# A mixture-of-experts decoder step: the routing block is put in another order

## The chip, the cores and the metric

One core of a Trainium2 chip runs the whole program. The metric is the time on the device of one execution, in microseconds; three runs of the kernel before gave a median of 1024.52 us (1024.07 to 1025.87).

The core has five engines that run their own instruction lists side by side and meet at semaphores: TensorE (PE in the profile; its weight loads are PEld), VectorE (DVE), ScalarE (ACT), GpSimd (POOL) and SyncE (SP), which here only issues DMAs. PSUM, where matmul results land, has eight banks; the kernel calls them `bank[:, 0..7, :]`.

## The reference

One step of a one-layer decoder: 256 tokens of a prompt and 8 sample tokens. Attention and a state-space branch are merged, projected and added to the residual; then a mixture of experts with a shared expert follows. The change lies between the merged branches and the experts:

```python
m = merged @ p['w_out']
x = x + g1 * rms_norm(m, p['g_post_mix'])
h = rms_norm(x, p['g_pre_ffn']) * (1 + sc2) + sh2
scores = sigmoid(h @ p['w_router'])          # 64 experts, in 8 groups of 8
biased = scores + p['b_router']              # the 4 best groups by their two best, then 6 experts
# w = scores of the 6, normalised, times 2.5
routed = sum over the chosen experts of w * (silu(h @ gate_e) * (h @ up_e)) @ down_e
shared = (silu(h @ w_gate_s) * (h @ w_up_s)) @ w_down_s
x = x + g2 * rms_norm(routed + shared, p['g_post_ffn'])
```

`rms_norm` needs the sum of squares over the 1024 channels of a token. All is float32. An expert has 3.15 MB of weights (2.1 MB gate and up, 1.05 MB down), and all 64 are read.

## The kernel before, in words

The program is a row of blocks. In each, every engine has its list; at the end of a block each engine drains (a `DRAIN` at the block's own line in the profile), and the next block starts for all when the last has. Three blocks matter: the merge (L1397), the **routing block** (L1580) and the **expert block** (L1951).

**Routing block.** Tokens are in three tiles: tile 0 and tile 2 of the router (in the code `j` = 0 and 1) are the prompt's two halves of 128, and tile 1 of the router are the 8 samples.

- TensorE projects (L1621): for each `j`, two halves of 512 output channels, one bank each, eight k-steps. The samples have their own projection (L1654, L1660) and sums of squares (L1628) ahead and between.
- For each `j` ScalarE squares the 1024 channels of a token with a running sum and takes the root (L1710, L1712); VectorE takes the reciprocal, scales and adds the residual (L1762 to L1765); ScalarE squares again; VectorE scales and shifts (L1770 to L1773). That is `h2`, tokens in partitions.
- TensorE turns `h2` in 128 x 128 pieces into banks 6 and 7 (L1634), ScalarE copies them to `h2t` (L1733, L1744), TensorE multiplies by the router's weights (L1639), ScalarE applies the sigmoid (a table switch ahead of it, L1736).
- VectorE's `route` (L1790 to L1823) finds groups, experts and ranks by max-8 and match-replace instructions and leaves a `key` per token and expert, tile 0 and the samples in one call and tile 2 in a second. TensorE turns the keys so that experts lie in partitions (L1690, L1691, L1696). `take_list` (L1832, L1838) then takes the 32 largest keys of each expert in four rounds of eight, on 64 partitions for tile 0 and samples, later on the other 64 for tile 2. The two lists are interleaved, multiplied by a parity column (L1854) and turned into slot tables (L1698, L1703, L1857 to L1865).
- Between these TensorE computes the shared expert's gate and up products in pieces (`shared`, L1646): for the first 128 tokens (`shared(.., 0, P)`, four pieces of 16 matmuls) and for the other 136 (four more). Silu and a product follow (L1749, L1868).
- GpSimd stores `h2` and the samples' rows to DRAM (L1605 to L1609), waits for those stores and for the tables, and issues the first two gathers (L1537), each of the 128 tokens of an expert pair.
- SyncE loads weights of the experts 0 to 4 into five slots. Experts 0 and 1 at once; the others when their space is free: after the last projection (L1586 on, `t_done`), after `h2` is done (`h2_ready`), and expert 4's gate and up weights after the second last shared piece has been computed (`sgu_done`).

**Expert block.** For each expert TensorE turns gathered tokens (L2038), multiplies by gate and up (L2128), by down (L2054), and adds the weighted rows (L2065). SyncE loads expert e + 5 when expert e has been multiplied (L1527, L1532). The order of the work is written out by hand everywhere.

Of the kernel before, what the change touches and what calls it, by code (L numbers as in the profile page):

```python
# [16 lines left out]
ALU = mybir.AluOpType  # L17
ACT = mybir.ActivationFunctionType
AX = mybir.AxisListType

P = 128
# [89 lines left out]
for _name, _n in (("ident", P), ("ones", P), ("eps", 1), ("causal_t", P), ("before", P), ("mask", P), ("cos", T), ("sin", T),  # L111
                  ("valid", NT), ("later", NBLK - NE),
                  ("count", MAXOVER), ("same_head", NH), ("code", NT), ("parity", 2), ("pair", NE // 2)):
    CONSTS[_name] = (_at, _at + _n)
    _at += _n
# [11 lines left out]
def build(nc, io):  # L127
    with ExitStack() as top:
# [1360 lines left out]
        with ExitStack() as moe:  # L1489
# [52 lines left out]
            with ExitStack() as ph:  # L1542
# [14 lines left out]
                listed_f = sb("listed_f", [P, 2 * HB], stack=ph)  # L1557
                listed_p = sb("listed_p", [P, 2 * HB, 2], stack=ph)
                ss = sb("ss", [P, 4], stack=ph)
# [5 lines left out]
                dummy = sb("spare", [P, 1], stack=ph)  # L1565
# [13 lines left out]
                sg_ready9, paired = sem("sg_ready9", ph), sem("paired", ph)  # L1579
                with nc.Block() as block:  # L1580
                    @block.sync
                    def _(sp):
# [6 lines left out]
                        sp.wait_ge(t_done, 2)  # L1589
# [3 lines left out]
                        sp.wait_ge(h2_ready, 2)  # L1593
# [5 lines left out]
                    def _(pool):  # L1599
# [4 lines left out]
                        pool.wait_ge(h2_ready, 1)  # L1604
# [3 lines left out]
                        pool.wait_ge(h2_ready, 2)  # L1608
# [9 lines left out]
                    def _(pe):  # L1618
                        def token_tile(j, h):
                            for k in range(KD):  # L1620
                                mm = pe.matmul(bank[:, 2 * j + h, :], merged[:, k, j * P:(j + 1) * P], w_out[:, k, h * 512:(h + 1) * 512],  # L1621
                                               start=(k == 0), stop=(k == KD - 1))
                            if h:
                                mm.then_inc(t_done, 1)

# [5 lines left out]
                        def turn_tile(j):  # L1631
                            pe.wait_ge(h2_ready, j + 1)
                            for k in range(KD):
                                mm = pe.transpose(bank[:, 6 + k // 4, k % 4 * P:(k % 4 + 1) * P], h2[:, j, k * P:(k + 1) * P], ident)  # L1634
                            mm.then_inc(tr_done, 1)

                        def logits(out, lo, n):
                            for k in range(KD):
# [5 lines left out]
                        def shared(half, i, lo, n):  # L1644
                            for k in range(KD):
# [11 lines left out]
                        token_tile(0, 0)  # L1657
# [28 lines left out]
                        pe.wait_ge(tr_took, 2)  # L1686
                        logits(bank[:, 4, 0:NE], P, P).then_inc(logits_done, 1)
                        shared(1, 1, 0, P)
                        pe.wait_ge(key_ready, 1)
                        pe.transpose(bank[0:NE, 5, 256:256 + P], key[:, 0, :], ident)  # L1690
                        pe.transpose(bank[0:NE, 5, 256 + P:256 + P + TS], key[0:TS, 1, :], ident[0:TS, 0:TS]).then_inc(key_done, 1)  # L1691
                        for i in range(2):
                            shared(0, i, P, T - P)
                            shared(1, i, P, T - P).then_inc(sgu_done, 1)
                        pe.wait_ge(key_ready, 2)
                        pe.matmul(bank[NE:2 * NE, 4, 0:P], key[:, 2, :], ident, start=True, stop=True).then_inc(key_done, 1)  # L1696
# [3 lines left out]
                        for l in range(2):  # L1700
                            for q in range(2):
                                lo = l * LB + q * HB
                                mm = pe.matmul(bank[lo:lo + HB, 7, 0:NE // 2], listed_f[:, l::2], ident[:, l * NE + q:(l + 1) * NE:2],  # L1703
                                               start=True, stop=True)
                        mm.then_inc(tab_done, 1)

                    @block.scalar
                    def _(act):
                        def square(i, src):
                            act.activation(junk, src, ACT.Square, accum_out=ss[:, i:i + 1]).then_inc(ss_ready, 1)  # L1710
                            act.wait_ge(ss_ready, i + 1)
                            act.activation(rt[:, i:i + 1], ss[:, i:i + 1], ACT.Sqrt, bias=eps, scale=1.0 / D).then_inc(rooted, 1)  # L1712
# [903 lines left out]
```

## Time and profile before

| | |
|---|---|
| median of 3 runs | 1024.52 us |
| profiled execution: time | 1025.71 us |
| profiled execution: span | 1023.8 us |
| TensorE busy | 947.5 us (93%) |
| VectorE busy | 342.5 us (33%) |
| ScalarE busy | 193.0 us (19%) |
| GpSimd busy | 119.7 us (12%) |
| DMA moved | 320.07 MB, mean 313 GB/s |
| routing block | 441.3 to 511.1 us |
| expert block | 511.1 us to the end |

The profile is of one execution; its span lies inside its time, which is 1.9 us longer. "Busy" counts instructions of an engine, and matmuls are pipelined, so that a full TensorE is not one at its peak. Names of tiles are the program's; a tile placed over another's space shows under that name (`h` for `h2`, `x` for `h2t`, `ring`, `slot_b`, `done_out` and `row_of` for expert weights). A float32 matmul shows as two.

### The profile page before, as it was taken

To read this page: it belongs to the slowest core of one execution; us is meant where nothing else is said; L and a number is where in the kernel's file an instruction comes from. 1 tells how busy PE (TensorE), PEld (TensorE's weight loads), DVE (VectorE), ACT (ScalarE), POOL (GpSimd) and SP (SyncE) were. 2 spreads that over 40 slices of the span, in tenths; PEclk is the share of its full clock that TensorE was granted. 3 is DMA by queue.
4 is the path that set the end of the run, shared out by engine and by line. 5 is a ranking of instruction groups with operands and counts; after the bars stand their busy time and mean duration, and the time that the engine had idled before them with its cause. 6 is when DMAs were issued, how large, how long until landed. Compare 5 with 4: busy or idle time off the path is not lost. (4 is left out here: it accounts for less than half of the span.)

```text
span 1023.8 us, 18759 instructions
## 1 busy us (share of the span) xinstructions
PE 947.5 (93%) x7777; PEld 584.0 (57%) x7777; DVE 342.5 (33%) x850; ACT 193.0 (19%) x465; POOL 119.7 (12%) x148
## 2 busy tenths in 40 slices
PE   4899999998998679999599999999999999999997
PEld 3788888875565447856554544444445444544442
DVE  0433840065444864515522222211122122122124
ACT  1100110334221690004111111111011111111112
POOL 0000000052561000000001111101011111011000
PEclk8999999998998797999889999999999999999999
DMA  9794857272794867076579999999999999999961
GB/s 375 293 351 179 311 203 314 82 279 78 269 334 174 340 229 303 1 310 261 204 263 402 426 422 420 418 421 419 396 404 424 420 421 396 424 421 420 413 236 51
DMA packets 56151, 320.07 MB, mean 313 GB/s; under 512 B 14881, under 2 KB 24818, under 8 KB 35138
## 3 DMA queue, kind: packets, MB, share of 16 engines
q1 hardware_dynamic: 43282, 300.20, 72.8%
q0 software_dynamic: 11056, 18.47, 5.3%
q8 instruction: 63, 1.03, 0.4%
q10 hardware_dynamic: 1728, 0.18, 0.1%
q14 instruction: 22, 0.18, 0.0%
HBM read 321.32 MB, written 15.71 MB: 329 GB/s over the span
## 5 line engine op out<-in xcount | busy, mean ns | idle before, releaser
L366 PE MATMUL bank<-h,ring 128*128 128x264 f32 x672 | 154.3, 390 | 2.4 <-DVE h L244 1.8
L366 PEld LDWEIGHTS bank<-h,ring 128*128 128x128 f32 x672 | 127.7, 191 | 26.5 <-issue 3.0
L2354 DVE TENSOR_TENSOR hh<-sge,bank 64x256 f32<-64x256 f32 x64 | 27.1, 423 | 227.6 <-ACT sge L2256 227.6
L2256 ACT ACTIVATE sge<-bank 64x256 f32<-64x256 f32 x64 | 24.2, 377 | 415.7 <-PE bank L2128 415.7
L2128 PE MATMUL bank<-done_out,xt 128*64 128x256 f32 x832 | 95.6, 382 | 0.0
L2128 PE MATMUL bank<-ring,xt 128*64 128x256 f32 x800 | 93.3, 386 | 0.8 <-ACT xt L2247 0.8
L2299 DVE COPY sq<-bank 128x512 f32<-128x512 f32 x64 | 44.3, 692 | 106.1 <-PE bank L2054 106.1
L1537 POOL DMA_INDIRECT xg<-tok_rows,tab_g x32 | 31.9, 998 | 374.3 <-PE bank L2038 354.2
L2054 PE MATMUL bank<-ring,ht 128*32 128x512 f32 x400 | 72.8, 598 | 1.8 <-DMA ring<-in_w_e 1.8
L2128 PEld LDWEIGHTS bank<-done_out,xt 128*64 128x64 f32 x832 | 58.6, 138 | 27.1
L2128 PEld LDWEIGHTS bank<-ring,xt 128*64 128x64 f32 x800 | 56.9, 140 | 27.8 <-issue 2.1
L2065 PE MATMUL bank<-sq,wmat 64*128 64x512 f32 x256 | 72.1, 640 | 0.0
L2038 PE MATMUL bank<-con,xg 128*128 128x128 f32 x256 | 42.8, 291 | 8.6 <-PEq L1580 7.8
L2054 PE MATMUL bank<-slot_b,ht 128*32 128x512 f32 x208 | 49.7, 598 | 0.7 <-DMA done_out<-in_w_e 0.7
L2054 PE MATMUL bank<-done_out,ht 128*32 128x512 f32 x208 | 49.5, 598 | 0.6 <-DMA row_of<-in_w_e 0.6
L2054 PE MATMUL bank<-row_of,ht 128*32 128x512 f32 x208 | 49.5, 598 | 0.0
L2065 PEld LDWEIGHTS bank<-sq,wmat 64*128 64x128 f32 x256 | 19.4, 184 | 52.6 <-issue 51.1
L2128 PE MATMUL bank<-slot_b,xt 128*64 128x256 f32 x416 | 47.8, 382 | 0.0
L2038 PEld LDWEIGHTS bank<-con,xg 128*128 128x128 f32 x256 | 27.3, 142 | 32.8 <-issue 32.8
L2362 DVE COPY ht<-bank 128x128 f32<-128x128 f32 x64 | 24.7, 387 | 59.4 <-PE bank L2168 59.3
L2247 ACT COPY xt<-bank 128x512 f32<-128x512 f32 x64 | 37.5, 586 | 26.5 <-PE bank L2038 26.5
L254 PE MATMUL bank<-ring,sc 128*32 128x128 f32 x768 | 26.6, 297 | 15.6 <-DMA ring<-in_w_units 14.4
(473 smaller groups left out, 1204.6 us busy)
## 6 DMA issues: line engine op xcount, KB each, us to landing
ring<-in_w_units SPq DMA_DIRECT2D x28, 2048.0 KB, 10.4
done_out<-in_w_e SPq DMA_DIRECT2D x26, 2048.0 KB, 16.7
ring<-in_w_e SPq DMA_DIRECT2D x25, 2048.0 KB, 16.5
slot_b<-in_w_e SPq DMA_DIRECT2D x13, 2048.0 KB, 18.1
ring<-in_w_e SPq DMA_DIRECT2D x25, 1024.0 KB, 17.1
slot_b<-in_w_e SPq DMA_DIRECT2D x13, 1024.0 KB, 17.7
done_out<-in_w_e SPq DMA_DIRECT2D x13, 1024.0 KB, 16.5
row_of<-in_w_e SPq DMA_DIRECT2D x13, 1024.0 KB, 16.7
```

The lines of the kernel that those rows point to most:

```text
L254: mm = pe.matmul(bank[32 * g:32 * g + 32, b, (u % 4) * P:(u % 4 + 1) * P], sc[:, k, :], w[:, k, g, :], start=(k == 0), stop=(k == KD - 1))
L366: mm = pe.matmul(bank[:, t % NB, 0:T], w[:, j, k, :], h[:, k, :], start=(k == 0), stop=(k == KD - 1))
L1537: pool.indirect_dma_start(xg[q % AHEAD][:, :], None, tok_rows, bass.IndirectOffsetOnAxis(ap=tab_g[:, q:q + 1].bitcast(U32), axis=0), bound ...
L2038: mm = pe.transpose(bank[:, 5, i * P:(i + 1) * P], xg[q % AHEAD][:, k * P:(k + 1) * P], ident)
L2054: mm = pe.matmul(bank[lo:lo + HB, b, :], ht[e % 4][:, k, l * HB:(l + 1) * HB], dn_w[e % SLOTS][:, k, h * 512:(h + 1) * 512], start=(k == 0 ...
L2065: mm = pe.matmul(bank[:, 2 * l + h, :], wmat[q % 2][at, :], yo[q % NYO][at, h * 512:(h + 1) * 512], start=(q == 0), stop=(q == NPAIR - 1))
L2128: mm = pe.matmul(bank[c * LB:(c + 1) * LB, 4, 0:FE], xt[e // 2 % 2][:, k, e % 2::2], gu_w[e % SLOTS][:, k, c * FE:(c + 1) * FE], start=(k ...
L2247: act.copy(xt[q % 2][:, KD // 2 * h:KD // 2 * (h + 1), :], bank[:, 5, :].rearrange("p (k n) -> p k n", n=P)).then_inc(xt_ready, 1)
L2256: act.activation(sg[e % 2][:, :], bank[0:LB, 4, 0:FE], ACT.Silu).then_inc(sg_ready, 1)
L2299: dve.tensor_copy(yo[q % NYO][:, h * 512:(h + 1) * 512], bank[:, b, :]).then_inc(y_ready, 1)
L2354: dve.tensor_tensor(hh[e % 2][:, :], sg[e % 2][:, :], bank[LB:2 * LB, 4, 0:FE], ALU.mult).then_inc(hh_ready, 1)
L2362: dve.tensor_copy(ht[e % 4][:, :, :].rearrange("p k (l r) -> p k r l", l=2), bank[:, 7, 0:2 * LB].rearrange("p (k r l) -> p k r l", k=2, l ...
```

## The change

The same results are computed by the same engines, in another order and in other pieces:

- Projection: each half is issued in two parts of four k-steps, `low` and `high`, and the samples' work is put between them. The samples' logits and their transposes stand between the two parts of the third half.
- Norms: squares, scales and additions by half rows. The sum of the first half, divided and with epsilon added (`first`), is the bias of the root over the second half's. The gain is multiplied in ahead of the reciprocal.
- Turns of `h2`, copies and logits by halves.
- Routing in three calls: samples, tile 0, tile 2. ScalarE switches its tables to sigmoid, back to sqrt and to sigmoid again.
- Both lists in one: keys of tile 2 lie in partitions 64 to 127 of the same bank as the others, and `take_lists` takes both at once. The parity column becomes four columns `side`; in the last round the multiply by them comes between the max-8 and the match-replace.
- The key turns stand ahead of most shared pieces. The last half piece and the four of 136 columns stand behind the tables.
- Waits of the loads: `t_done` counts halves (4), `h2_ready` counts halves and is waited for at 3 instead of the whole.

```diff
-                        sp.wait_ge(t_done, 2)
+                        sp.wait_ge(t_done, 4)
-                        sp.wait_ge(h2_ready, 2)
+                        sp.wait_ge(h2_ready, 3)
-                        pool.wait_ge(h2_ready, 1)
+                        pool.wait_ge(h2_ready, 2)
-                        pool.wait_ge(h2_ready, 2)
+                        pool.wait_ge(h2_ready, 4)
...
-                        token_tile(0, 1)
+                        token_part(0, 0, high)
                         sample_sums(0)
-                        token_tile(1, 0)
+                        token_part(0, 1, low)
                         pe.wait_ge(s_summed, 1)
                         sample_sums(1)
-                        token_tile(1, 1)
-                        turn_tile(0)
+                        token_part(0, 1, high)
+                        token_part(1, 0, low)
                         pe.wait_ge(w_r_in, 16)
-                        pe.wait_ge(tr_took, 1)
                         pe.wait_ge(h2s_ready, 1)
-                        logits(bank[:, 5, 64:128], 0, P)
-                        logits(bank[0:TS, 5, 128:192], TP, TS).then_inc(logits_done, 1)
+                        logits(bank[0:TS, 5, 128:192], TP, TS, range(KD)).then_inc(s_logits, 1)
                         for k in range(KD):
                             mm = pe.transpose(bank[0:TS, 6 + k // 4, k % 4 * P:(k % 4 + 1) * P], h2t[:, k, TP:T], ident)
                         mm.then_inc(srow_done, 1)
+                        token_part(1, 0, high)
+                        token_part(1, 1, range(KD))
+                        pe.wait_ge(srow_took, 1)
+                        turn_half(0, 0)
+                        turn_half(0, 1)
+                        pe.wait_ge(score_ready, 2)
+                        pe.wait_ge(tr_took, 1)
+                        logits(bank[:, 5, 64:128], 0, P, low)
+                        pe.wait_ge(tr_took, 2)
+                        logits(bank[:, 5, 64:128], 0, P, high).then_inc(logits_done, 1)
                         wait_unit(pe, U_SGU)
-                        pe.wait_ge(x1_ready, 1)
-                        for i in range(2):
-                            shared(0, i, 0, P)
-                        pe.wait_ge(srow_took, 1)
-                        turn_tile(1)
                         pe.wait_ge(x1_ready, 2)
+                        shared(0, 0, 0, P, low)
+                        turn_half(1, 0)
+                        turn_half(1, 1)
+                        pe.wait_ge(tr_took, 3)
+                        logits(bank[:, 4, 0:NE], P, P, low)
+                        pe.wait_ge(tr_took, 4)
+                        logits(bank[:, 4, 0:NE], P, P, high).then_inc(logits_done, 1)
+                        pe.wait_ge(x1_ready, 4)
+                        shared(0, 0, 0, P, high)
+                        pe.matmul(bank[NE:2 * NE, 5, 256 + P:256 + P + TS], ident[0:TS, NE:2 * NE], ident[0:TS, 0:TS], start=True, stop=True)
+                        pe.wait_ge(key_ready, 2)
+                        pe.transpose(bank[0:NE, 5, 256:256 + P], key[:, 0, :], ident)
+                        pe.transpose(bank[0:NE, 5, 256 + P:256 + P + TS], key[0:TS, 1, :], ident[0:TS, 0:TS])
+                        shared(0, 1, 0, P)
+                        pe.wait_ge(key_ready, 3)
+                        pe.matmul(bank[NE:2 * NE, 5, 256:256 + P], key[:, 2, :], ident, start=True, stop=True).then_inc(key_done, 1)
                         shared(1, 0, 0, P)
...
+                        shared(1, 1, 0, P, low)
                         pe.wait_ge(paired, 1)
...
+                        shared(1, 1, 0, P, high)
+                        for i in range(2):
+                            shared(0, i, P, T - P)
+                            shared(1, i, P, T - P).then_inc(sgu_done, 1)
...
+                        def row_root(i):
+                            act.wait_ge(ss_ready, 2 * i + 2)
+                            act.wait_ge(first_ready, i + 1)
+                            act.activation(rt[:, i:i + 1], ss[:, 2 * i + 1:2 * i + 2], ACT.Sqrt, bias=first[:, i:i + 1], scale=1.0 / D
+                                           ).then_inc(rooted, 1)
...
+                        act.activation(dummy[:, 2:3], eps, ACT.Sqrt)
+                        mixed_rows(1)
+                        take_turned(0)
+                        residual_rows(1)
+                        act.activation(dummy[:, 3:4], eps, ACT.Sigmoid)
+                        act.wait_ge(logits_done, 1)
+                        act.activation(score[:, 0, :], bank[:, 5, 64:128], ACT.Sigmoid).then_inc(score_ready, 1)
+                        take_turned(1)
...
+                        def mix(j):
+                            for h in range(2):
+                                dve.wait_ge(ss_ready, 4 * j + h + 1)
+                                dve.tensor_tensor(h2[:, j, part_of(h)], bank[:, 2 * j + h, :], row_of[:, 0, part_of(h)], ALU.mult).then_inc(gained, 1)
+                                if h == 0:
+                                    first_half(2 * j)
                         def residual(j):
                             dve.wait_ge(rooted, 2 * j + 1)
                             link(dve.reciprocal(rt[:, 2 * j:2 * j + 1], rt[:, 2 * j:2 * j + 1]))
+                            for h in range(2):
+                                dve.wait_ge(gained, 4 * j + h + 1)
+                                dve.scalar_tensor_tensor(x_rows[:, j, part_of(h)], h2[:, j, part_of(h)], rt[:, 2 * j:2 * j + 1],
+                                                         x_rows[:, j, part_of(h)], ALU.mult, ALU.add).then_inc(x1_ready, 1)
...
+                        def take_lists():
+                            dve.wait_ge(key_done, 1)
+                            src = bank[:, 5, 256:256 + P + TS]
+                            for r in range(HB // 8):
+                                best = listed_f[:, 8 * r:8 * r + 8]
+                                ins = dve.max(best, src if r == 0 else work[:, :])
...
+                                ins = dve.match_replace(work[:, :], best, src if r == 0 else work[:, :], 0.0)
                         sample_sum(0)
-                        residual(0)
                         sample_scale(0, bank[:, 5, 0:KD * TS].rearrange("p (k t) -> p k t", k=KD), samp[:, 0, :, :], x[:, :, TP:T],
                                      x1_s[:, :, :], x1s_ready)
-                        modulate(0)
                         sample_sum(1)
                         sample_scale(1, x1_s[:, :, :], samp[:, 1, :, :], mod[:, 24:32, 1:ROWS], h2t[:, :, TP:T], h2s_ready)
+                        mix(0)
+                        residual(0)
+                        modulate(0)
+                        route(0, 1, 2)
+                        mix(1)
                         residual(1)
                         modulate(1)
-                        route(0, 0, 2)
-                        take_list(0, bank[0:NE, 5, 256:256 + P + TS], 0, P + TS)
-                        route(1, 2, 3)
-                        take_list(1, bank[NE:2 * NE, 4, 0:P], NE, P)
+                        route(1, 0, 1)
+                        route(2, 2, 3)
+                        take_lists()
```

## Rows read from the trace of the kernel before

**Rows 1.** Stages: length, busy per engine (instructions), granted clock, DMA share, GB/s.
```profile
504.00:511.00 7.00, 0.00 (x0) 0.00 (x0) 1.40 (x6) 0.00 (x0) 2.07 (x2) 0.50 0.46 155
511.00:518.00 7.00, 5.29 (x25) 3.47 (x27) 0.00 (x0) 1.17 (x2) 0.99 (x1) 0.53 0.17 36
...
540.00:900.00 360.00, 360.00 (x2916) 175.16 (x2917) 81.94 (x197) 44.34 (x92) 44.77 (x47) 1.00 1.00 416
```
**Rows 2.** The chain that ended last: start, us, what; its last weight transfer.
```profile
943.55 22.92 DMA done_out<-in_w_e
```
**Rows 3.** Timeline of SyncE's queue: start, us; the sixth expert's load.
```profile
519.93 0.33 SPq L1527 DMA_DIRECT2D ring<-in_w_e  x1
```
**Rows 4.** The routing block's own line: drains, duration in ns, start in us.
```profile
L1580 PEldq DRAIN  x1: 633/633/633, 502.8 to 502.8; - x1
L1580 DVEq DRAIN  x1: 783/783/783, 504.8 to 504.8; - x1
L1580 POOLq DRAIN  x1: 6106/6106/6106, 504.8 to 504.8; - x1
```
**Rows 5.** Timeline of GpSimd: start, us, idle before and releaser; both gathers.
```profile
504.48 1.06 POOL L1537 DMA_INDIRECT xg<-tok_rows,tab_g  x1 [19.73 <-DVE tab_g L1858]
505.85 1.01 POOL L1537 DMA_INDIRECT xg<-tok_rows,tab_g  x1 [0.30 <-issue]
```
**Rows 6.** Timeline of TensorE, 467 to 530 us.
```profile
467.84 7.09 PE L1621 MATMUL bank<-w_out,merged 128*128 128x512 f32 x16
...
491.30 7.68 PE L1646 MATMUL bank<-x,ring 128*128 128x136 f32 x64
...
502.74 0.41 PE L1698 MATMUL bank<-con,listed_p 128*128 128x32 f32 x2 [3.39 <-DVE listed_p L1854]
...
511.18 1.09 PE L2038 MATMUL bank<-con,xg 128*128 128x128 f32 x4 [7.83 <-PEq L1580]
...
514.88 5.02 PE L2128 MATMUL bank<-ring,xt 128*64 128x256 f32 x32 [0.77 <-ACT xt L2247]
...
526.08 3.68 PE L2128 MATMUL bank<-done_out,xt 128*64 128x256 f32 x32
```
**Rows 7.** Groups of TensorE by form, 441 to 511: busy us, mean ns.
```profile
L1639 PE MATMUL bank<-w_r,x 128*8 128x64 f32 x16 | 1.1, 219 | 0.0
L1676 PE MATMUL bank<-con,x 128*8 128x128 f32 x8 | 1.0, 273 | 0.0
```
**Rows 8.** Timeline of VectorE.
```profile
482.38 1.22 DVE L1773 TENSOR_TENSOR h<-h,row_of 128x1024 f32<-128x1024 f32 x1
...
491.41 0.30 DVE L1832 MAX8 listed_f<-bank 64x8 f32<-64x136 f32 x1 [2.47 <-PE bank L1691]
...
493.98 0.28 DVE L1838 MATCH_REPLACE8 work<-listed_f,work 64x136 f32<-64x136 f32 x1
...
497.58 0.28 DVE L1823 SCALAR_TENSOR_TENSOR key<-rank,con,chosen 128x64 f32<-128x64 f32 x1
```
**Rows 9.** Groups of ScalarE by form, 441 to 511.
```profile
L1710 ACT ACTIVATE sq<-bank 128x1024 f32<-128x1024 f32 x2 | 2.1, 1028 | 11.9 <-PE bank L1621 11.9
...
L1710 ACT ACTIVATION_READ_ACCUMULATOR sq<-bank 128x1 f32 x2 | 0.4, 195 | 0.0
```
**Rows 10.** Timeline of ScalarE: a table load and what follows.
```profile
480.77 1.28 ACT L1736 ACT_TABLE_LOAD   x1
482.07 0.20 ACT L1736 ACTIVATE spare<-con 128x1 f32<-128x1 f32 x1
```
**Rows 11.** DMA issues, 484 to 485: KB, us to landing.
```profile
tok_rows<-h POOLq DMA_DIRECT2D x1, 512.0 KB, 10.6
```
**Rows 12.** Line L1537, all 32 gathers.
```profile
DMA to landing us min/median/max: 3.7/10.5/11.6
```
**Rows 13.** Stage, columns as in rows 1.
```profile
388.00:395.00 7.00, 6.19 (x21) 5.39 (x21) 4.37 (x9) 0.26 (x1) 0.00 (x0) 0.50 0.77 281
```
**Rows 14.** Timeline of TensorE, after two other block ends.
```profile
388.81 3.86 PE L1428 MATMUL bank<-o_attn,ring 128*128 128x264 f32 x8 [1.02 <-PEq L1081]
...
441.35 3.68 PE L1654 MATMUL bank<-w_out,root 128*32 128x512 f32 x32 [1.54 <-PEq L1397]
```

More of the change, by code:

```diff
@@ L112 @@
                   ("valid", NT), ("later", NBLK - NE),
-                  ("count", MAXOVER), ("same_head", NH), ("code", NT), ("parity", 2), ("pair", NE // 2)):
+                  ("count", MAXOVER), ("same_head", NH), ("code", NT), ("side", 4), ("pair", NE // 2)):
     CONSTS[_name] = (_at, _at + _n)
@@ L1629, in sample_sums, with turn_half, logits @@
                                       ).then_inc(ones_done, 1)
[L1631 to L1634, printed above, removed]
+                        def turn_half(j, h):
+                            pe.wait_ge(h2_ready, 2 * j + h + 1)
+                            for k in range(4):
+                                mm = pe.transpose(bank[:, 6 + h, k * P:(k + 1) * P], h2[:, j, (4 * h + k) * P:(4 * h + k + 1) * P], ident)
                             mm.then_inc(tr_done, 1)
-                        def logits(out, lo, n):
-                            for k in range(KD):
+                        def logits(out, lo, n, ks):
+                            for k in ks:
                                 mm = pe.matmul(out, h2t[:, k, lo:lo + n], w_r[:, k, :], start=(k == 0), stop=(k == KD - 1))
@@ L1642, in _, with shared @@
                         w_sgu = unit(U_SGU, "p (j k c) -> p j k c", j=4, k=KD, c=P)
-                        def shared(half, i, lo, n):
-                            for k in range(KD):
+                        def shared(half, i, lo, n, ks=range(KD)):
+                            for k in ks:
                                 mm = pe.matmul(bank[:, 2 * half + i, lo:lo + n], w_sgu[:, 2 * half + i, k, :], h2t[:, k, lo:lo + n],
@@ L1688, in _ @@
[L1688 to L1695, printed above, removed]
@@ new lines, in residual_rows, with take_turned @@
+                        def residual_rows(j):
+                            for h in range(2):
+                                act.wait_ge(x1_ready, 2 * j + h + 1)
+                                square_half(4 * j + 2 + h, x_rows[:, j, part_of(h)])
+                            row_root(2 * j + 1)
+                        def take_turned(j):
+                            for h in range(2):
+                                act.wait_ge(tr_done, 2 * j + h + 1)
+                                act.copy(h2t[:, 4 * h:4 * h + 4, j * P:(j + 1) * P], bank[:, 6 + h, :].rearrange("p (k t) -> p k t", t=P)
+                                         ).then_inc(tr_took, 1)
@@ L1755, in _, with first_half @@
                         dve.memset(gx[:, :, NG:], SENT)
-                        dve.memset(ex[:, :, NE:], SENT)
-                        dve.memset(listed_f[:, :], 0.0)
-                        link(dve.memset(work[:, :], 0.0))
+                        link(dve.memset(ex[:, :, NE:], SENT))
+                        def first_half(i):
+                            dve.wait_ge(ss_ready, 2 * i + 1)
+                            dve.tensor_scalar(first[:, i:i + 1], ss[:, 2 * i:2 * i + 1], 1.0 / D, EPS, ALU.mult, ALU.add).then_inc(first_ready, 1)
+                        def mix(j):
+                            for h in range(2):
+                                dve.wait_ge(ss_ready, 4 * j + h + 1)
+                                dve.tensor_tensor(h2[:, j, part_of(h)], bank[:, 2 * j + h, :], row_of[:, 0, part_of(h)], ALU.mult).then_inc(gained, 1)
+                                if h == 0:
+                                    first_half(2 * j)
                         def residual(j):
@@ L2577, in constants @@
     put("code", NOWHERE + 1 - 8 * tok)
-    put("parity", r[:, None] % 2 == np.arange(2)[None, :])
+    put("side", 2 * (r[:, None] // NE) + r[:, None] % 2 == np.arange(4)[None, :])
     put("pair", r[:, None] % NE // 2 == np.arange(NE // 2)[None, :])
```

94 lines of the change are left out of this document (44 added, 50 removed).

## The prediction

> **What bounds the kernel now.** I read the stages first [rows 1], then the chain of waits near its end [rows 2]. From 540 to 900 us both TensorE and the DMA engines are full (360 of 360 us, share 1.00, 416 GB/s). This is the expert stage. Its weights are 59 experts of 3.15 MB behind the five that fit in the slots, 185.6 MB; at 416 GB/s that is 446 us. The load of the sixth expert is issued at 519.93 [rows 3], and the last transfer of the chain lands at 943.55 + 22.92 = 966.5 us [rows 2]: 446.5 us. So the stream is saturated from its first free slot on, and that slot comes free when expert 1 has been multiplied. Whatever lets expert 0 start earlier moves the stream and the end by the same amount. Nothing of the change lies behind that point.
>
> Expert 0 starts when the routing block ends. There the view to read is the block's own last instructions [rows 4]: TensorE's drain ends at 503.4, VectorE's at 505.6, but GpSimd's runs from 504.8 to 510.9, and TensorE starts the next block at 511.18 [rows 6]. GpSimd issued its two gathers at 504.48 and 505.85 [rows 5]; its drain ends 5.05 us after the second began. TensorE meanwhile idles, its granted clock is at the lower level (0.50, 1.2 GHz of 2.4) from 504 to 511, and still mostly there (0.53) from 511 to 518 [rows 1]. So the path is: last projection of token tile 1, norms, router, lists, gathers, drain, expert 0.
>
> **The change, step by step** (times on the axis of the trace).
>
> *TensorE before the norms.* The eight sample logits (1.1 us) and eight sample transposes (1.0 us) [rows 7] move ahead of the second half of the projection. They overlap their neighbours, so I charge 1.2 + 0.9 = 2.1 us. Projection ends at 467.84 + 7.09 = 474.93 now [rows 6], at 477.05 after. Bounds: 0 (if they filled a wait; but this stretch has none) and 2.1.
>
> *Norms of tile 1.* Now: 474.95 to the end of the modulation, 482.38 + 1.22 = 483.60 [rows 8], 8.65 us. After, only half a row is left when the projection ends. ScalarE squares 512 instead of 1024 elements (1.03 us and 0.20 for the sum now [rows 9], so 0.5 to 0.55 and 0.20 after), and the root, then on VectorE: gain multiply, reciprocal, two half scale-adds, two half gain multiplies with a 0.16 us scalar between, reciprocal, two half scale-adds. A row-wide VectorE instruction is 1.22 us [rows 8], so halves are 0.65 to 0.69 (an estimate: half, and some start-up): 0.75 + 0.69 + 0.17 + 1.33 + 1.46 + 0.17 + 1.33 and 0.1 of hops = 6.0 us. That is 2.65 shorter. h2 of tile 1 is ready at 477.05 + 6.0 = 483.05, against 483.60. ScalarE's two copies of tile 0 (0.55 each) lie beside the first scale-adds.
>
> *Router.* The samples' tile is routed at about 467 to 470, while VectorE waits for the projection: free (3.6 us if that cover went). What remains is one tile at a time. One tile takes from the end of a list, 493.98 + 0.28 = 494.26, to 497.58 + 0.28 = 497.86: 3.6 us [rows 8]. Now VectorE routes two tiles together, waits for TensorE, takes list 0 from 491.41 to 494.26, routes the third tile, waits again and takes list 1; the tables start at 502.74 [rows 6], 19.1 us behind the norms. After: 483.05 + 2 x 3.6 = 490.2. The scores must be there: ScalarE reloads its sigmoid table in this stretch, 1.28 us [rows 10], 481.15 to 482.4, scores at 482.8, so just hidden behind VectorE. The two added table loads are this one's pair (sqrt again, at about 468, in a wait) and it: together 2.56 us of ScalarE, path 0 to 0.3. Tile 2's logits: turned 483.0 to 483.6, copied to 484.3, multiplied to 485.5, well before VectorE wants them at 486.6.
>
> A rule speaks against this step. The row shows 1.28 us and the next instruction right behind it. The Trainium skill (ScalarE: Activation LUTs, What ACT_TABLE_LOAD costs) gives some 1283 ns for the load, which agrees, and a drain of some 1380 ns more at each switch, which this trace does not show. By the page the scores would be 1.4 us later and the sum about 1.1 us worse; I go by the row.
>
> *Lists.* One list for 128 partitions instead of two for 64: 2.85 us falls off (the first and the last of its 12 instructions stand in the group) [rows 8], the last round's replace is moved behind the pair multiply (0.4), and the 128 x 128 pair multiply costs 0.35 instead of about as much now. Key transpose 490.2 to 490.65, list to 493.15, pair 493.5, tables 493.5 (now 502.74), gather index 494.4. TensorE does two shared pieces less a half meanwhile (2.8 us), so it is there at 493.4. The lists are thus 9.2 us earlier. This is not the gain.
>
> *GpSimd's end.* The first gather stands 504.48 - 502.74 = 1.74 us behind the tables now [rows 5, 6], so 495.3 after; the second 496.7, drain end 501.7. But the store of tile 1's rows must have landed. It took 10.6 us behind the weight loads [rows 11]; those are now issued 2.1 us later, so it lands between 483.1 + 10.6 = 493.7 and 496.9. In the later case the drain ends at 503.9 or so.
>
> *TensorE's end.* The shared pieces that used to stand before the lists now stand behind them: one half (0.9) and the four of 136 columns, 7.68 us for 64 matmuls [rows 6]. So 493.5 + 0.6 (tables) + 0.9 + 7.6 = 502.7, then Silu 0.4, the product 0.4, drain: 503.6 to 503.9. **This takes over from GpSimd as what ends the block.** I take 504.2 for the start of the next, between 503.8 and 505.5 (a wait of TensorE mis-seen by a microsecond). Gain: 511.18 - 504.2 = 7.0 us.
>
> *The clock.* Now expert 0's 32 matmuls take 5.02 us against 3.68 for expert 2's, and each of the two turns ahead of them 1.09 [rows 6], of which I put 0.4 to the clock: 2.1 us for the lower level. After, TensorE is idle for 1.5 us at the block's end instead of 7.8. The gap of 1.54 at the block's end at 441 was followed by matmuls of full pace (32 in 3.68 us) [rows 14]. But it is also little used in the next 3 us (two short turns and two copies). I take half, 1.05; ends 0 and 2.1.
>
> *Loads.* Expert 4's gate weights wait for the shared pieces and are issued at 502.8 instead of 499.0: 2.1 MB, 5 us, done at 508 to 510. The sixth expert's load comes at 504.2 + 7 = 511. DMA stands nearly idle there now (share 0.17 in 511 to 518 [rows 1]), so nothing; up to 3 us if they meet.
>
> **Sum.** 7.0 + 1.05 = 8.05. The profiled execution (span 1023.8, time 1025.71) would become 1017.7; it lies 1.2 above the median of 1024.52, and the median becomes **1016.5**. Own range: 1024.52 - 7.0 - 2.1 = 1015.4 to 1024.52 - (511.18 - 505.5) = 1018.8.
>
> **Rivals.**
> 1. *GpSimd's drain still ends the block.* A gather usually lands 10.5 us after issue [rows 12], not the 4.2 of the quiet end. For: the row store and expert 3's weights are still in the queues at 495. Against: they are gone by 497. If the second gather starts at 498.3 and drains 8 us later, the block ends at 506.5: gain 4.65, clock half lost, about 0.5: 1019.4.
> 2. *The clock falls inside routing.* TensorE now waits three times (478, 481.4, 488.8; 1 to 1.4 us each). For: 388 to 395 ran at 0.50 though TensorE was busy in 6.19 of the 7 us [rows 13]; the lower clock can hold on through full work. Against: after the gap of 1.54 at 441 it did not fall [rows 14]. At the lower clock eight matmuls of 264 columns take 3.86 us [rows 14], 1.8 ns a column; at the upper one 64 of 136 columns take 7.68 [rows 6], 0.9 ns: twice the time. If it stays low for 8 us, 4 us of work are added: block end 508.2, gain 3: 1021.5.
> 3. *Slower: the same, but to the end.* From 490.6 TensorE has 12 us of work until its last shared piece, formerly done in the shadow of VectorE's lists. All of it at the lower clock ends the block at 516, 5 us later than now: 1029.5. It decides from 7 us of stretched work on, that is where the clock falls before 495 and doesn't recover. Against: TensorE is nearly full from 490 on, and the clock recovered within 7 us of the start at 511 [rows 1].
> 4. *The change does not carry.* The weight stream, not the start, sets the end: 1024.5. For: the share of 1.00 from 540 to 900. Against: 185.6 MB at 416 GB/s fill exactly the time from 519.93, so it starts with the block.
>
> **Chances.** Forecast 0.63, rival 1 0.15, rival 2 0.12, rival 3 0.04, rival 4 0.06. Range: 1014.5 (0.9 below the full-clock sum, for a half microsecond of mis-sized terms on either side) to 1021.5 (rivals 1 and 2 in). A change below 0.2% (2 us) can't be told from none here. Faster 0.91, same 0.05, slower 0.04.
>
> **What would show it.** Right: GpSimd's drain ends before TensorE's in the routing block; the next block starts at 504 to 505; tables at 493 to 494; norms of tile 1 6 us after the last projection; TensorE's last shared piece at 502 to 503; expert stage of unchanged length. Wrong: a GpSimd drain that ends last (rival 1), a granted clock of 0.50 between 478 and 503 (2 or 3), or an expert stage longer by what the block gained (4).

## The result and the profile after

The changed kernel takes 1013.94 us (median of 6 runs, 1007.74 to 1017.03), the kernel before beside it 1024.21 (6 runs, 1022.42 to 1025.87): ratio 0.9897, 95% interval [0.9871, 0.9923]. The direction and the mechanism were as forecast. The size was not: 10.3 us instead of 8.05, and the median of 1013.94 lies 0.6 us below the range. Two slow executions, one of the kernel before at 1914.08 us and one of two_lists at 1041.81, are left out of all ratios and medians.

The profiled execution has a span of 1011.9 us, a time of 1013.63. First its stages, columns as in [rows 1].

```profile
481.00:484.00 3.00, 2.98 (x25) 2.50 (x24) 2.69 (x20) 1.43 (x4) 0.57 (x1) 1.00 0.94 396
484.00:488.00 4.00, 3.55 (x29) 3.08 (x28) 3.58 (x23) 1.51 (x2) 0.00 (x0) 1.00 1.04 430
...
492.00:501.00 9.00, 8.90 (x82) 8.61 (x81) 1.71 (x10) 0.46 (x2) 2.07 (x2) 1.00 0.36 122
501.00:505.00 4.00, 1.38 (x10) 0.99 (x12) 0.43 (x1) 1.50 (x3) 0.11 (x1) 1.00 0.82 266
505.00:512.00 7.00, 6.66 (x60) 4.70 (x61) 2.53 (x10) 0.96 (x2) 0.88 (x1) 1.00 0.82 304
512.00:880.00 368.00, 367.96 (x2988) 179.70 (x2985) 83.98 (x204) 46.19 (x96) 45.03 (x47) 1.00 1.00 414
```

The stretch of 7 us without a matmul [rows 1] is gone, and the granted clock is 1.00 right through. The expert stage is as full as before. TensorE's timeline, the counterpart of [rows 6]:

```profile
465.12 10.46 PE L1627 MATMUL bank<-w_out,merged 128*128 128x512 f32 x24
...
488.42 0.43 PE L1711 MATMUL bank<-con,key 128*64 128x128 f32 x2 [0.87 <-DVE key L1878]
488.78 2.94 PE L1654 MATMUL bank<-x,ring 128*128 128x128 f32 x24
491.79 0.41 PE L1715 MATMUL bank<-con,listed_p 128*128 128x32 f32 x2
...
492.32 8.57 PE L1654 MATMUL bank<-x,ring 128*128 128x128 f32 x72
502.09 0.63 PE L2098 MATMUL bank<-con,xg 128*128 128x128 f32 x4 [1.19 <-PEq L1586]
503.48 0.63 PE L2098 MATMUL bank<-con,xg 128*128 128x128 f32 x4 [0.77 <-ACT xt L2307]
504.88 3.68 PE L2188 MATMUL bank<-ring,xt 128*64 128x256 f32 x32 [0.77 <-ACT xt L2307]
```

The block runs from 439.94 to 501.98, 62.0 us; before it ran from 441.24 to 511.07, 69.8. The tables start 51.9 us into it (61.5 before). Expert 0 takes 3.68 us instead of 5.02 and each turn 0.63 instead of 1.09; together 2.25 us. The drains at the end, as in [rows 4], and GpSimd's gathers, as in [rows 5]:

```profile
L1586 POOLq DRAIN  x1: 7069/7069/7069, 494.6 to 494.6; - x1
L1586 PEldq DRAIN  x1: 2275/2275/2275, 498.7 to 498.7; - x1
...
L1586 DVEq DRAIN  x1: 444/444/444, 501.4 to 501.4; - x1
```

```profile
494.34 1.06 POOL L1537 DMA_INDIRECT xg<-tok_rows,tab_g  x1 [12.14 <-DMA tok_rows<-h]
495.70 1.01 POOL L1537 DMA_INDIRECT xg<-tok_rows,tab_g  x1 [0.30 <-issue]
```

TensorE's is done at 501.0, GpSimd's at 501.7 and VectorE's, which waited for the Silu of the last piece, at 501.8. The first gather waited for the store of tile 1's rows, as the prediction had allowed for. Two views of VectorE and ScalarE, as in [rows 8] and [rows 10]: end of the norms, last keys; the table load.

```profile
479.93 1.41 DVE L1827 SCALAR_TENSOR_TENSOR h<-h,rt,row_of 128x512 f32<-128x512 f32 x2
...
488.08 0.28 DVE L1878 SCALAR_TENSOR_TENSOR key<-rank,con,chosen 128x64 f32<-128x64 f32 x1
```

```profile
479.65 1.28 ACT L1781 ACT_TABLE_LOAD   x1
480.95 0.20 ACT L1781 ACTIVATE spare<-con 128x1 f32<-128x1 f32 x1
481.06 0.20 ACT L1783 ACTIVATE score<-bank 128x64 f32<-128x64 f32 x1
```

### The profile page after: what moved, and what is told of

It is laid out like the page before. It is cut to its first block, busy times and chain, and to the rows that moved or that the text cites. A ratio compares the mean times of both kernels' runs of the same rounds, so it can differ in the third digit from the quotient of the medians.

```text
span 1011.9 us, 18784 instructions
## 1 busy us (share of the span) xinstructions
PE 945.0 (93%) x7779; PEld 582.0 (58%) x7779; DVE 341.5 (34%) x850; ACT 196.9 (19%) x479; POOL 119.7 (12%) x148
## 4 chain that ended last, share of the span: by engine, by line
PE 47%; DMA 2%; DVE 1%; ACT 0%; issue 0%; DVEq 0%
PE bank L2188 22%; PE bank L2114 11%; PE bank L2125 6%; PE bank L2098 3%; DMA done_out<-in_w_e 2%; PE bank L2228 1%; PE bank L2135 1%; PE bank L2176 1%; PE bank L2161 0%; DVE slot_b L2524 0%; PE bank L2154 0%; DVE slot_b L2519 0%; ACT slot_b L2333 0%; DVE slot_b L2530 0%; ACT xt L2307 0%
## 5 line engine op out<-in xcount | busy, mean ns | idle before, releaser
L1537 POOL DMA_INDIRECT xg<-tok_rows,tab_g x32 | 31.9, 998 | 363.8 <-PE bank L2098 351.3
```

Source lines behind the costliest of these rows:

```text
L1537: pool.indirect_dma_start(xg[q % AHEAD][:, :], None, tok_rows, bass.IndirectOffsetOnAxis(ap=tab_g[:, q:q + 1].bitcast(U32), axis=0), bound ...
```

## The experiments

Times vary by several us between executions, more than most single steps are worth. So each trace is also split in parts: start of the routing block, its length, the 32 matmuls of expert 0, and the rest of the span behind them (the two turns, 0.63 us each at the upper clock and 1.09 at the lower, stand between block and expert 0). The table has one trace of each kernel; all but "us" and "ratio" are us in that one trace, "tables at" from the block's start. "Gathers" is from the second gather's start to the end of GpSimd's drain; "us" is the median of the executions (4 to 12 of each kernel), and "ratio" is to the kernel before, run beside it on the same chip: its medians there were 1024.21 for the changed kernel, 1023.39 for again, warm_before, late_end and filled, 1023.9 for shared_first, order_alone, two_lists and two_tiles, and 1023.11 for again2, order_late4, warm_after and best.

| kernel | us | ratio, 95% interval | start | block | tables at | gathers | expert 0 | rest |
|---|---|---|---|---|---|---|---|---|
| before | 1024.21 | | 441.2 | 69.8 | 61.5 | 5.1 | 5.02 | 503.9 |
| changed | 1013.94 | 0.9897 [0.9871, 0.9923] | 439.9 | 62.0 | 51.9 | 6.0 | 3.68 | 503.3 |
| again | 1011.85 | 0.9882 [0.9852, 0.9913] | 437.3 | 62.0 | 51.8 | 5.9 | 3.68 | 505.8 |
| again2 | 1011.60 | 0.9905 [0.9873, 0.9938] | 436.7 | 62.0 | 51.9 | 6.0 | 3.68 | 503.2 |
| warm_before | 1020.94 | 0.9975 [0.9951, 0.9998] | 438.5 | 70.4 | 61.5 | 4.9 | 3.68 | 503.2 |
| late_end | 1022.09 | 0.9988 [0.9965, 1.0010] | 442.3 | 68.9 | 51.9 | | 5.40 | 502.9 |
| shared_first | 1023.73 | 0.9997 [0.9976, 1.0018] | 439.9 | 69.8 | 59.9 | 6.6 | 4.97 | 504.7 |
| order_alone | 1023.27 | 1.0005 [0.9989, 1.0020] | 437.1 | 70.9 | 58.7 | 8.9 | 6.10 | 503.7 |
| order_late4 | 1019.86 | 0.9968 [0.9947, 0.9990] | 437.1 | 67.0 | 58.7 | 5.0 | 6.42 | 503.5 |
| two_lists | 1020.04 | 0.9968 [0.9945, 0.9990] | 438.4 | 67.0 | 56.9 | 4.9 | 5.12 | 502.6 |
| two_tiles | 1015.16 | 0.9900 [0.9864, 0.9936] | 439.0 | 63.9 | 53.7 | 5.0 | 5.01 | 503.8 |
| filled | 1012.66 | 0.9896 [0.9862, 0.9930] | 437.0 | 60.4 | 51.9 | 5.0 | 6.58 | 504.1 |
| warm_after | 1013.30 | 0.9914 [0.9886, 0.9942] | 437.3 | 62.0 | 51.9 | 5.0 | 3.68 | 502.9 |
| best | 1011.31 | 0.9901 [0.9865, 0.9936] | 438.4 | 60.4 | 51.9 | 5.1 | 3.68 | 503.7 |

**again** and **again2**: the changed kernel, nothing edited.

> The changed kernel, unchanged. Its six runs so far lie between 1007.7 and 1017.0 us and its median fell 10.3 us, 2.2 more than forecast. Theory C (clock and end of block): the routing block again takes 62 us (before: 69.9) and expert 0's 32 matmuls run at the upper clock (3.7 us, before: 5.0); what differs between runs is the granted clock in earlier blocks (386 to 401 us). Median ratio 0.990, gain 10 us. Rival D (the extra came by chance): the first expert shows 5.0 us in this trace, and the gain is 8 us or less.

> The changed kernel once more, beside the next three. Its two traces so far have expert 0 at the upper clock (3.7 us); variants of it with the same end of the block had 5.0, 5.1 and 6.6. Theory C': with TensorE idle for 1.2 us and little used for the 3 us behind it, the clock holds in some executions only, so runs differ by up to 3 us from this alone; block 62 us as before. Median 1012 to 1014. Rival: always 3.7.

Block and expert 0 are the same in all three traces. The rest is 2.5 us longer in again; in that trace the granted clock falls once more near the end of the expert block (0.83 from 950 to 960, 1.00 in the other two), and how much of the 2.5 us this makes is not shown. Expert 0 was at the upper clock three times of three; that it varies is not seen here, but it is in variants below.

**warm_before**

```diff
+                        for k in range(28):
+                            pe.matmul(bank[:, 4, 256:256 + P], ident, ones, start=True, stop=True)
```

> The kernel before, with 28 extra matmuls of 128 columns on TensorE behind the slot tables, results not read, so that it is busy from 503.4 to about 510 while GpSimd drains. Nothing else is moved. Theory C: the granted clock does not fall at 504, expert 0's matmuls take 3.7 instead of 5.0 us and the two turns 0.65 instead of 1.09; the block still ends at GpSimd's drain, 69.9 us long, and the program is 2.2 us faster (1022.0 against 1024.2). Rival: the clock costs nothing there because the weight stream sets the end; same time as before.

The extra matmuls, the turns and expert 0 of this kernel:

```profile
500.54 8.15 PE L1707 MATMUL bank<-con 128*128 128x128 f32 x56
...
508.98 0.63 PE L2040 MATMUL bank<-con,xg 128*128 128x128 f32 x4 [0.30 <-PEq L1580]
...
511.77 3.68 PE L2130 MATMUL bank<-ring,xt 128*64 128x256 f32 x32 [0.77 <-ACT xt L2249]
```

The upper clock is back, though the block got 0.5 longer (the extra matmuls, partly at the lower clock, ended 0.6 us behind GpSimd's drain). By the medians the kernel is 2.4 us faster than before beside it, a ratio of 0.9975 whose interval just excludes 1. That fits a clock price of 2.25 us that reaches the end of the program (1.7 with the longer block taken off); the interval, 0.2 to 5 us, is too wide to measure the price itself.

**late_end**

```diff
                         for e in range(2):
                             gather(pool, e)
+                        for e in range(11):
+                            pool.memset(junk, 0.0).then_inc(cleared, 1)
+                            pool.wait_ge(cleared, e + 3)
```

> The changed kernel with 11 extra memsets of 1.0 us on GpSimd behind the two gathers, into space that nobody reads any more: the block ends some 6.3 us later with TensorE idle for 7 us, as it was before the change. Theory C: +6.3 us for the end of the block and +2.2 us for the lower clock in expert 0 (5.0 us instead of 3.7), together 8.5 us slower than the changed kernel, about 1022.5. If the end of the block alone counts: +6.3. If the weight stream has slack that swallows a later start: less than +3.

```profile
511.33 1.08 PE L2101 MATMUL bank<-con,xg 128*128 128x128 f32 x4 [8.05 <-PEq L1586]
...
515.03 5.40 PE L2191 MATMUL bank<-ring,xt 128*64 128x256 f32 x32 [0.77 <-ACT xt L2310]
```

The block is 6.9 longer, turns and expert 0 cost 2.6 more, 9.5 together; the median is 10.2 above again's of the same chip, and the rest of the trace is no shorter than the changed kernel's (502.9 against 503.3). A later start is passed on in full, which rules out rival 4.

**shared_first**

```diff
-                        shared(1, 1, 0, P, low)
+                        shared(1, 1, 0, P)
+                        for i in range(2):
+                            shared(0, i, P, T - P)
+                            shared(1, i, P, T - P).then_inc(sgu_done, 1)
                         pe.wait_ge(paired, 1)
...
-                        shared(1, 1, 0, P, high)
-                        for i in range(2):
-                            shared(0, i, P, T - P)
-                            shared(1, i, P, T - P).then_inc(sgu_done, 1)
```

> The changed kernel with the last half piece and the four pieces of 136 columns of the shared expert put back ahead of the slot tables (behind the last key turn). Theory A (what the change moves off the path is the wait of the lists and tables for TensorE): the tables wait for 8.5 us of matmuls and start at 500.3 instead of 491.8; first gather 1.7 behind them at 502, GpSimd's drain ends at 508.5 to 509, block 69 us instead of 62, TensorE idle for 7 us, so the lower clock in expert 0 too: 9 us slower than the changed kernel, about 1023. Rival B (the gain is the shorter vector chain: halves, one list, samples first): 2 us slower or less.

With halves, one list and early samples in place but the shared pieces ahead of the tables, nothing is left of the gain. The tables come 8.1 us later. The gathers also took 0.6 us more than in the changed kernel; here expert 4's load stands 2.9 us ahead of the second one (500.07 and 502.96), so not quite all of the 7.7 us is TensorE's order.

**order_alone** and **order_late4**: the kernel before with TensorE's order alone; then also with the load of expert 4's gate and up weights moved from the end of SyncE's list in the routing block to the start of its list in the expert block.

```diff
                         logits(bank[:, 4, 0:NE], P, P).then_inc(logits_done, 1)
-                        shared(1, 1, 0, P)
                         pe.wait_ge(key_ready, 1)
...
+                        shared(1, 1, 0, P)
+                        shared(0, 0, P, T - P)
+                        shared(1, 0, P, T - P).then_inc(sgu_done, 1)
                         pe.wait_ge(key_ready, 2)
...
+                        shared(0, 1, P, T - P)
...
+                        shared(1, 1, P, T - P).then_inc(sgu_done, 1)
```

> The kernel before with TensorE's order alone changed: the key turns stand ahead of the shared pieces, one piece of 136 columns stands behind the tables; norms, routing and lists are as before. Theory A: VectorE's waits of 2.5 and 1.5 us for the key turns shrink to 0.5 each, tables at 499.8 instead of 502.7, GpSimd's drain still ends the block at 508.2: 3 us of the block, no clock gain (TensorE idle for 6 us): 1021.3. Theory B expects under 1 us from this.

The tables came 2.8 us earlier as expected, and the block got 1.1 us longer, where 3 us less had been expected. SyncE's queue, GpSimd and its drain in order_alone:

```profile
498.46 0.33 SPq L1527 DMA_DIRECT2D ring<-in_w_e  x1
```
```profile
498.89 1.01 POOL L1537 DMA_INDIRECT xg<-tok_rows,tab_g  x1 [0.30 <-issue]
```
```profile
L1580 POOLq DRAIN  x1: 10023/10023/10023, 497.8 to 497.8; - x1
```

> The kernel order_alone with the 2.1 MB load of expert 4 issued at the start of the expert block instead of in the routing block. In order_alone the tables came 2.8 us earlier, but the load was issued 0.4 us ahead of the second gather, GpSimd's drain ended 8.9 us behind that gather's start instead of 5.05 and the block was 1.0 us longer than before. Theory (the gathers share the DMA queues with the load): the drain ends 5.0 us behind the second gather again, block 67 us, 2.9 shorter than before, 1.5 to 3 us faster in time. Rival (the drain waits for something else, TensorE's or SyncE's work): block 70.9 again.

The same two rows of order_late4:

```profile
498.90 1.01 POOL L1537 DMA_INDIRECT xg<-tok_rows,tab_g  x1 [0.30 <-issue]
```
```profile
L1580 POOLq DRAIN  x1: 6087/6087/6087, 497.8 to 497.8; - x1
```

The second gather starts at the same place in both, and the drain ends at 507.8 in the one, at 503.9 in the other. The load was all that differed: a 2.1 MB load issued 0.4 us ahead of the second gather costs the block 3.9 us. With it out of the way TensorE's order alone is worth 2.8 us of the block. In the changed kernel that load comes 5.2 us behind the second gather (500.93) and does no harm.

**two_lists**

```diff
+                        take_list(0)
                         route(2, 2, 3)
-                        take_lists()
+                        take_list(1)
```

> The changed kernel with the two lists taken one after the other, 64 partitions each: list 0 between the two routings. Theory: 2.9 us more on VectorE, plus 0.5 for the first key turn's wait: tables at 495.1 instead of 491.8, TensorE's last piece and the block's end 3.3 us later; TensorE idles for 3 us at 491 but not behind the block, so the clock stays: 3.3 us slower than the changed kernel, block 65.3. If TensorE's shared pieces alone set the end, less than 1.

It cost 5.0, not 3.3, and the 3.3 came as 3.7 (the last key turn starts 52.2 us into the block instead of 48.5). TensorE idles for 4.6 us at the last key turn, and the clock falls inside the block; its timeline, then its stages:

```profile
490.54 0.51 PE L1711 MATMUL bank<-con,key 128*64 128x128 f32 x2 [4.56 <-DVE key L1878]
490.98 4.46 PE L1654 MATMUL bank<-x,ring 128*128 128x128 f32 x24
```
```profile
487.00:490.00 3.00, 0.00 (x0) 0.00 (x0) 2.65 (x20) 0.00 (x0) 0.00 (x0) 1.00 0.92 388
490.00:495.00 5.00, 4.46 (x24) 4.21 (x25) 3.42 (x15) 0.00 (x0) 0.00 (x0) 0.66 0.39 166
```

The 24 matmuls that take 2.94 us in the changed kernel take 4.46, and the tables wait for them: 1.4 us. That is rival 2, in miniature.

**two_tiles**

```diff
-                        route(0, 1, 2)
...
-                        route(1, 0, 1)
+                        route(1, 0, 2)
```

> The changed kernel with the samples routed together with token tile 0 again, behind the norms of tile 1, instead of in VectorE's wait for the projection. Theory: two tiles together take 5.4 us where one takes 3.5, so keys, lists, tables and the block's end come 1.9 us later: block 63.9, 1.9 us slower. If VectorE's chain is not what TensorE's last pieces wait for: 0.

1.8 us of the block, as expected: VectorE's chain is passed on to TensorE's last piece. The first turn and expert 0:

```profile
502.97 0.63 PE L2097 MATMUL bank<-con,xg 128*128 128x128 f32 x4 [1.19 <-PEq L1586]
...
505.76 5.01 PE L2187 MATMUL bank<-ring,xt 128*64 128x256 f32 x32 [0.77 <-ACT xt L2306]
```

TensorE's gap at the block's end is 1.19 us, as in the changed kernel, and yet the clock falls (0.51 from 505 to 508.5).

**filled**, **warm_after** and **best**: further than the change. In filled a whole first piece stands before the turns of tile 1, `shared(1, 0, 0, P)` before the last key turn, half a piece of 136 columns before the tables, and the load of expert 3's down weights behind the shared pieces.

```diff
+                        sp.wait_ge(sgu_done, 2)
                         load_dn(sp, 3)
-                        sp.wait_ge(sgu_done, 2)
...
-                        shared(0, 0, 0, P, low)
+                        shared(0, 0, 0, P)
                         turn_half(1, 0)
...
+                        shared(1, 0, 0, P)
                         pe.wait_ge(key_ready, 3)
```

> The changed kernel with one more piece moved: TensorE's waits at 480 and 487.6 us are filled with half pieces and a whole piece of the shared expert, and the load of expert 3's down weights is issued after the shared pieces instead of at 480.7, so that the store of token tile 1 lands before the gather wants it. In the trace of the changed kernel the block ended at GpSimd's drain (501.67) and VectorE's (501.84) at once, and the first gather waited for the store until 494.3. Theory: gathers 0.7 us earlier, TensorE's last piece 1.0 to 1.4 us earlier, the block 0.8 to 1.2 us shorter (61 us), the program about 1 us faster. Rival: GpSimd's drain does not follow the gather but stays, and the block is at most 0.2 us shorter.

The block is 1.6 us shorter, more than the 0.8 to 1.2 expected, but this trace lost 2.9 us in expert 0, with a granted clock of 0.53 from 499 to 506:

```profile
497.51 0.63 PE L2098 MATMUL bank<-con,xg 128*128 128x128 f32 x4 [1.33 <-PEq L1586]
...
500.30 6.58 PE L2188 MATMUL bank<-ring,xt 128*64 128x256 f32 x32 [0.77 <-ACT xt L2307]
```

warm_after adds four unread matmuls behind the last piece and three behind each turn; best is filled with these and with the load of expert 4's gate weights at the start of the expert block.

> The changed kernel with ten extra matmuls of 128 columns whose results are not read: four behind the last shared piece (0.9 us, while ScalarE, VectorE and GpSimd end the block) and three behind each of the two turns ahead of expert 0 (0.7 us, while ScalarE copies). Theory C': the clock holds in every execution, expert 0 takes 3.7 us, block 62.0 to 62.4; the median is 0 to 1.5 us below that of the changed kernel. Rival: the extra matmuls are on the path and it is 1 to 2 us slower.

> The kernel filled (block 60.4 us) with expert 4's load issued at the start of the expert block and the ten extra matmuls of warm_after: everything that paid so far. Theory: block 60.4, expert 0 at the upper clock, 1.6 us faster than warm_after and 1.6 to 3 faster than the changed kernel: 1010 to 1011. If it is not faster than the changed kernel by 1 us, the weight stream (expert 4's 5 us moved behind the block's end) takes it back.

In both the clock stays and the block keeps its length (62.0, 60.4). That the extra matmuls hold the clock is not shown by warm_after, for it held in the three traces of the changed kernel too. Neither median can be told from again2's 1011.60 on the same chip. Warm_after missed its expectation of a gain: it is 1.7 us above, the rival's number, but not for the rival's reason, for expert 0 starts 64.9 us behind the block's start in both traces. Best is 0.3 us faster where 1.6 to 3 were expected; its expert 0 starts 63.3 us behind the block's start, the shortest way with the upper clock, but that it is the faster kernel is not shown.

## Why the prediction was right and wrong

Point by point, against the start of the block (so projection end is 35.8 us in the prediction):

- *What bounds the kernel.* Right: an earlier or later expert 0 moves the end by as much (the rest is 503.9 before, 503.3 changed, 502.9 in late_end). A slip without effect: the slot that comes free at 519.93 is that of expert 0, whose matmuls end at 514.88 + 5.02 = 519.90, not of expert 1.
- *Mechanism.* Right. The path was lists, gathers, drain. The gain needs both halves of the change: the shared pieces out of the way of keys and tables, and the shorter vector chain. The vector steps without the order gave nothing (shared_first: 7.7 of the 7.8 us of the block lost again), the order without the vector steps gave 2.8 (order_late4), and with the order in place the vector steps are passed on (two_tiles 1.8, two_lists 3.7 before its clock effect). No run undid the norms by halves alone.
- *TensorE before the norms.* Forecast 35.8, measured 475.58 - 439.95 = 35.6.
- *Norms.* Forecast 6.0, measured 481.34 - 475.58 = 5.8.
- *Router.* Two tiles in 7.15, measured 488.36 - 481.34 = 7.0. The third table load was hidden: load 1.28 us, the next instruction right behind, scores at 481.26, before the norms end. The 1.38 us that the Trainium skill adds to a switch (ScalarE: Activation LUTs, What ACT_TABLE_LOAD costs) is not in this trace either.
- *Lists and tables.* Key to tables 3.3, measured 3.4.
- *TensorE's end.* Tables to the end of the last piece 9.2, measured 500.89 - 491.79 = 9.1.
- *End of the block.* From there to the next block 1.5, measured 1.2. What takes over was named as TensorE's last piece. It is that, through ScalarE and VectorE (501.84), but only just: GpSimd's drain ended 0.17 us earlier (501.67), 0.06 us earlier in again and at the same time in again2. Its gathers took 5.9 to 6.0 us in all three traces of this kernel against a forecast of 5.0. In warm_after, where the first gather waited for the store too, they took 5.0; why is open.
- *Sum of the block.* Forecast 7.0, measured 7.8. Six terms, each off by 0.1 to 0.3, five of them the same way. This is the smaller part of the miss.
- *The clock: the step that failed.* "I take half, 1.05; ends 0 and 2.1." All of it came, 2.25 us, in three traces of three. The mechanism and its price were right, the middle between two outcomes was the wrong value to put in a sum, for here an execution kept the clock or lost it. That none of the three traces had the other is in part luck. Of the four kernels with a gap of 1.2 to 1.3 us at the block's end and nothing put into it, the changed one held the clock in all its traces and two_tiles, two_lists and filled lost it in their one trace each; what decides stays open. Where it fell there, the price in expert 0 was not one number either: 1.3 us (two_tiles), 1.4 (two_lists) and 2.9 (filled).
- *What that makes of the sum.* With both terms as measured, 7.8 + 2.25 = 10.05, the forecast would have been 1024.52 - 10.05 = 1014.5, the very end of the range. Of the last 0.6 us, 0.3 is that the kernel before gave 1024.21 and not 1024.52 beside the changed one; the rest is unexplained and small against a spread of 9 us between the six executions. The later comparisons of the same two kernels gave 11.5 us twice (again, again2); the intervals of their ratios reach from 6 to 15 us and both hold 10.05.
- *Loads.* Right, and by more luck than argument. The prediction asked only whether expert 4's load would meet the sixth expert's. The costly meeting is with the gathers (order_alone, 3.9 us), which it didn't ask about for this load. In the changed kernel the load comes behind the last shared piece (500.93, the piece ends at 500.89; `sgu_done` is counted after both gate and up of a column block, so its second count is the last piece and not the second last), and so behind the gathers.
- *Rivals.* Rival 1 in its own form did not come, but its mechanism is real (order_alone). Rival 2 came in two_lists, for 1.4 us. Rival 3 did not come, and rival 4 is ruled out by late_end.

## What to carry to other kernels

Read what ends a block from the drains of its engines, then ask for every engine what stands in its list before the work that the last one waits for; work that nobody needs before the block's end belongs behind what the last engine waits for. In the changed kernel it then also fills TensorE's wait for the gathers, and the clock stays up. Before moving a step, look which DMA it moves next to the gathers. Where a term has two outcomes, forecast the likelier and put the other in the range, not the mean.

## What the runs showed of the hardware

- GpSimd's drain at a block's end lasts until its last indirect DMA has landed. From the start of that DMA the landing took 4.7 us in order_late4, 4.8 in before, 5.7 in the changed kernel and 8.7 in order_alone, and the drain ended after 5.0, 5.1, 6.0 and 8.9. It was 4.9 to 5.1 in eight traces, 5.9 to 6.0 in the three of the changed kernel, 6.6 with a 2.1 MB load issued 2.9 us ahead (shared_first) and 8.9 with one 0.4 us ahead.
- The clock fell after a gap of 1.33 us at the block's end followed by little work (filled), and after a gap of 1.19 us it fell in two kernels (two_tiles, two_lists) and held in another (the changed one, three traces). In filled it then stayed low for 5.9 of the 6.58 us of expert 0's full matmuls.
- The same instructions up to the routing block took 436.7 to 442.3 us in fourteen traces. In every one of them the granted clock is at the lower level for some 14 us that end between 397 and 403, though TensorE is busy in most of it (13.19 of 14 us from 388 to 402 in the kernel before, at 0.51). Other stretches at the lower clock before the block differ in number and length from trace to trace. The times go with the clock: the fastest of the changed kernel, 1007.74 us, had a mean granted clock of 0.986, the two slowest, 1016.42 and 1017.03, had 0.973 and 0.972. This spread is larger than most single steps tested here, which is why the parts of a trace, not the medians, carry the verdicts on steps.
